# GpSimd in VectorE's place: the low part of the split weights, from the input projection to the output projection

## What is computed

```python
def first_block(x, ...):
    n = _rms(h, norm_mix_w[l])
    z = n @ w_in[l]                                  # (528, 1024) @ (1024, 7168)
    q, k, v, glu, g_att, g_conv = jnp.split(z, splits, axis=-1)
    ...
    o = _diff_attention(q, k, v, lam, cid)           # 8 heads, two softmaxes each
    y_att = (_rms(o, subln_w[l]) * (1.0 - lambda_init)).reshape(b, lp, ATT_V)
    u = glu[..., :CONV_CH] * jax.nn.sigmoid(glu[..., CONV_CH:])
    u = _causal_dwconv(u, conv_dw_w[l], conv_dw_b[l])   # 31 taps over 1024 channels
    u = jax.nn.silu(_layernorm(u, conv_ln_w[l], conv_ln_b[l]))
    y_conv = u @ w_conv_out[l]
    m = jax.nn.sigmoid(g_att) * y_att + jax.nn.sigmoid(g_conv) * y_conv
    h = h + m @ w_out[l]
    ...
    # then a gated feed-forward with 3-tap convolutions, a norm,
    # and two layers of short convolution and retention (second_block)
```

## Time and profile before

| | us |
|---|---|
| median of 3 runs | 1806.2 |
| lowest and highest of them | 1805.16, 1809.17 |
| the profiled execution, its own time | 1807.76 |
| its span, first to last instruction | 1806.0 |
| TensorE busy | 1787.0 (99%) |
| VectorE busy | 1403.3 (78%) |
| ScalarE busy | 967.9 (54%) |
| GpSimd busy | 164.6 (9%) |
| mean granted TensorE clock | 0.998 of full speed |

### The profile page before, as it was taken

How to read it: one execution, slowest core, us unless ns; L and a number is a source line. 1 busy time by engine, 2 the same in 40 slices (tenths; PEclk the granted TensorE clock), 3 DMA queues, 4 the chain that set the end, 5 groups by cost and what they waited for, 6 DMA issues and landing times.

```text
span 1806.0 us, 31948 instructions
## 1 busy us (share of the span) xinstructions
PE 1787.0 (99%) x13222; PEld 1687.2 (93%) x13222; DVE 1403.3 (78%) x2464; ACT 967.9 (54%) x1894; POOL 164.6 (9%) x138
## 2 busy tenths in 40 slices
PE   9999999999999999999999999999999999999998
PEld 8999999978899989999889999999898999999987
DVE  5888898578756789969878996899357898689844
ACT  6223332568734446547556665667346566566632
POOL 0000000000000012011001211120000122122000
PEclk9999999999999999999999999999999999999999
DMA  5222222200132257566346876785332677577531
GB/s 193 96 75 93 94 86 80 94 24 25 64 107 73 80 136 165 133 160 144 108 117 146 173 159 139 157 170 127 117 94 71 127 167 161 139 156 168 124 117 70
DMA packets 247679, 213.42 MB, mean 118 GB/s; under 512 B 6646, under 2 KB 239919, under 8 KB 247534
## 3 DMA queue, kind: packets, MB, share of 16 engines
q1 hardware_dynamic: 180990, 178.34, 32.2%
q0 software_dynamic: 66528, 33.04, 14.9%
q10 hardware_dynamic: 16, 0.00, 0.0%
HBM read 209.26 MB, written 2.10 MB: 117 GB/s over the span
## 4 chain that ended last, share of the span: by engine, by line
PE 88%; DVE 6%; ACT 4%; DMA 1%; issue 1%; SPq 0%; DVEq 0%; ACTq 0%
PE ps L664 41%; PE ps L705 29%; PE ps L1313 6%; PE ps L1362 5%; DVE wlo L2350 2%; PE ps L893 1%; PE ps L1151 1%; PE ps L1126 1%; ACT p L1624 1%; ACT whi L1396 1%; DMA raw<-in_w_up_dram 1%; PE ps L1142 1%; PE ps L1154 1%; PE ps L918 1%; DVE y L2846 0%
## 5 line engine op out<-in xcount | busy, mean ns | idle before, releaser
L2350 DVE TENSOR_TENSOR wlo<-raw,whi 128x1024 fp32r<-128x1024 f32 (+1 forms) x363 | 438.7, 1214 | 203.9 <-ACT whi L1396 203.0
L1396 ACT ACTIVATE whi<-raw 128x1024 fp32r<-128x1024 f32 (+1 forms) x363 | 380.8, 1052 | 253.3 <-PE ps L664 107.1
L664 PE MATMUL ps<-nhi,whi 128*128 128x256 f32 (+3 forms) x1392 | 315.9, 290 | 1.5 <-DVE clo L2618 0.8
L664 PE MATMUL ps<-nhi,wlo 128*128 128x256 f32 (+3 forms) x1392 | 311.8, 288 | 0.0
L664 PE MATMUL ps<-nlo,whi 128*128 128x256 f32 (+2 forms) x1264 | 275.0, 287 | 0.0
L664 PEld LDWEIGHTS ps<-nhi,whi 128*128 128x128 f32 x1392 | 226.8, 189 | 5.2 <-DVE clo L2618 1.0
L664 PEld LDWEIGHTS ps<-nhi,wlo 128*128 128x128 f32 x1392 | 225.8, 189 | 2.1
L705 PE MATMUL ps<-thi,whi 128*128 128x256 f32 x784 | 225.2, 287 | 2.1 <-DVE wlo L2350 0.7
L705 PE MATMUL ps<-thi,wlo 128*128 128x256 f32 x784 | 221.6, 283 | 0.0
L705 PE MATMUL ps<-tlo,whi 128*128 128x256 f32 x784 | 221.4, 282 | 0.0
L705 PE MATMUL ps<-nhi,whi 128*128 128x256 f32 (+1 forms) x756 | 215.8, 285 | 0.0
(11 more groups left out here) (473 smaller groups left out, 3604.1 us busy)
## 6 DMA issues: line engine op xcount, KB each, us to landing
raw<-in_w_in_dram SPq DMA_DIRECT2D x90, 1024.0 KB, 5.9
raw<-in_w_up_dram SPq DMA_DIRECT2D x22, 1024.0 KB, 5.1
raw<-in_w_out_dram SPq DMA_DIRECT2D x20, 1024.0 KB, 5.1
s1t<-in_w_in_dram SPq DMA_DIRECT2D x49, 256.0 KB, 3.5
s1t<-in_w_in_dram POOLq DMA_DIRECT2D x49, 256.0 KB, 7.1
raw<-in_w_in_dram POOLq DMA_DIRECT2D x49, 256.0 KB, 4.7
raw<-in_w_down_dram SPq DMA_DIRECT2D x16, 512.0 KB, 3.4
raw<-in_w_conv_out_dram SPq DMA_DIRECT2D x4, 1024.0 KB, 5.2
```

Source lines behind the costliest of these rows:

```text
L664: mm = eng.matmul(o, w, m[:, k, a:b], start=begins, stop=final and n == len(ks) - 1 and i == 2)
L1396: eng.activation(hi, raw, ACT.Copy).then_inc(*A.up("hi", s))
L2350: eng.tensor_tensor(lo, raw, hi.bitcast(F), ALU.subtract).then_inc(*V.up("lo", s))
```

## The change

A set of slots, `BY_GPSIMD`, is defined: from 4 up to the first slot of the feed-forward, 72 (68 slots). For these VectorE's `low(s)` returns at once, and GpSimd makes the same subtraction of the same operands, `G("lo", s)`, after `A("hi", s)`. The two waits on the low part, TensorE's in `products` and SyncE's before a load, ask the function `low_in` which engine made it. GpSimd's zeroing of `v` and of the two small tiles keeps its waits and now stands between the subtractions of slots 25 and 26, and of 57 and 58.

```diff
+        BY_GPSIMD = range(4, next(r for r, (u, _, _) in enumerate(slots) if u == first_ffn))
...
+        def low_in(s):
+            return G("lo", s) if s in BY_GPSIMD else V("lo", s)
+
         def tensor_program(eng):
...
                                 if n == c == i == j == 0:
-                                    on.wait_ge(V("lo", s))
+                                    on.wait_ge(low_in(s))
...
             def low(s):
+                if s in BY_GPSIMD:
+                    return
                 u, n, _ = box_of(s)
                 hi, lo, raw = split_views(s)
                 on.wait_ge(A("hi", s))
...
-            on.wait_ge(T("keys"), A("square_x", 0))
-            eng.memset(V_[:, 0, :], 0.0).then_inc(*G.up("meta"))
-            for i in range(2):
-                on.wait_ge(T("gate", 15))
-                eng.memset(AT[i][:, 4, :], 0.0).then_inc(*G.up("at_rows", i))
+
+            for s in BY_GPSIMD:
+                u = slots[s][0]
+                if s == slots.index((12, BY_COL[0], False)) + 2:
+                    on.wait_ge(T("keys"), A("square_x", 0))
+                    eng.memset(V_[:, 0, :], 0.0).then_inc(*G.up("meta"))
+                elif s == slots.index((28, BY_COL[0], False)) + 2:
+                    for i in range(2):
+                        on.wait_ge(T("gate", 15))
+                        eng.memset(AT[i][:, 4, :], 0.0).then_inc(*G.up("at_rows", i))
+                hi, lo, raw = split_views(s)
+                on.wait_ge(A("hi", s))
+                eng.tensor_tensor(lo, raw, hi.bitcast(F), ALU.subtract).then_inc(*G.up("lo", s))
...
                     if n > 1:
                         on.wait_ge(V("second_sum", sevens[n - 2]), V("lo", slot_of[sevens[n - 2], 1]))
-                    on.wait_ge(V("lo", raw2_read))
+                    on.wait_ge(low_in(raw2_read))
...
                 if final and v:
-                    on.wait_ge(V("lo", s))
+                    on.wait_ge(low_in(s))
```

## The result

| | before | after |
|---|---|---|
| median of the runs shown now, us | 1807.41 | 1823.26 |
| lowest of them, us | 1805.16 | 1821.48 |
| the profiled execution, its own time, us | 1807.76 | 1822.59 |
| its span, us | 1806.0 | 1820.8 |

The ratio is 1.0085, with a 95% interval of 1.0065 to 1.0105: the change costs some 0.85%. Forecast were 1828 (21.9 us more) and slower. One of the four runs of after, 1851.82, was disturbed and is left out of the ratio; the median of the other three is 1822.59, 15.2 us above before.

What follows compares the result with a forecast made beforehand. TensorE, busy 99% of the span, was taken to bound the kernel. Mean 14.1, clock 1.5 and attention 6.3 sum to 21.9 us, which on the 1806.2 median makes 1828; range 1804 to 1845.

Steps and rivals of the forecast that it cites:

- the term that decided: Convolution and attention: GpSimd's and VectorE's two-input SBUF instructions exclude each other, 2.3 us held per subtraction; chance 0.62.
- the memset: Six taps beside a GpSimd memset kept 4.07 us, so its writes do not slow VectorE; its reads stayed untested.
- no harm: Rival: engines share SBUF freely or VectorE loses under 2 us per subtraction; 1805 to 1808, chance 0.25.
- faster: Rival: attention's 4.4 us of TensorE idle all come from VectorE and vanish; 1801.8, chance 0.08.
- VectorE never lets go: Rival: GpSimd's subtractions wait behind 60 taps in one piece, three pieces costing 30 us each; 1890, chance 0.05.
- GpSimd's subtraction, 2.25 us: Estimated length of one 1024-column GpSimd subtraction, priced from its memset and one-input instruction; bounds 1.23 and 2.9 us.
- Held per subtraction, 2.3 us: VectorE blocked 2.25 us plus 0.05 for the change of hands; TensorE then waits 14.1 us at the mean.
- The prediction's own formula: VectorE's work up to the mean, 128.5 + 33 g + (61.94 - 13.8 + 12 g - 72), against 194 us; g is time held.
- the threshold of 2.0: Time held per subtraction, in us, from which VectorE's lateness costs TensorE anything at the mean.
- The clock, 1.5 us: Behind the stall at the mean the granted clock may fall once, 3 us at 1.2 GHz, losing 1.5 us.
- Attention, 0.9 us a head: GpSimd's reading delays `p`, VectorE's chain has 1.9 more and 1.15 less; 6.3 us over seven heads.
- What cost nothing: Costed at nothing: GpSimd's lateness to TensorE, SyncE's loads 1.1 us later, and VectorE's lighter list before the mean.

Runs made afterwards that it cites:

- nobody: Changed kernel with the low parts of slots 4 to 71 made by no engine: 1805.98 us against 1806.72, ratio 0.9995.
- quarters: Changed kernel with each GpSimd subtraction split into four instructions of 256 elements a row: 1809.74 us against 1805.16, ratio 1.0025.
- Twice as many: Changed kernel with each GpSimd subtraction in slots 4 to 57 made two times, one after the other: 1929.89 us against 1805.16, ratio 1.0692.
- Paced: Changed kernel, but VectorE still waits for each high part where its own subtraction used to stand: 1827.28 us against 1807.48, ratio 1.0117.
- input only: Changed kernel with only the slots before 58 (input projection and gates) on GpSimd: 1811.97 us against 1806.72, ratio 1.0026.
- Attention only: Changed kernel with only the slots from 58 on (attention and output projection) on GpSimd: 1818.77 us against 1806.72, ratio 1.0064.
- attention late: Kernel with only slots from 58 on GpSimd; the heads' subtractions wait for VectorE's largest score: 1815.28 us against 1807.48, ratio 1.0047.
- the copy: Changed kernel with GpSimd copying the raw weights (one input) in place of subtracting: 1870.25 us against 1805.16, ratio 1.0359.
- every other: Changed kernel with alternate pairs of slots 4 to 57 on GpSimd, the rest back on VectorE: 1807.32 us against 1805.16, ratio 1.0012.

## Why the prediction was right where it was, and where not

**Direction and mechanism: right.** TensorE's full list left nothing to gain (*nobody*: 0.9995), and GpSimd's subtraction and VectorE's two-input instructions exclude each other, which was the term that decided. That for instructions with two inputs it is reading that excludes, as argued from the memset, is shown by the kernel that only writes. Of the rivals *no harm* and *faster* are out. *VectorE never lets go* is not what set the time of this kernel, but it is real: one subtraction in the changed kernel shows it.

```profile
245.40 10.72 DVE L2527 SCALAR_TENSOR_TENSOR c<-u,cv,c 128x514 f32<-128x514 f32 x16
...
256.42 2.15 DVE L2563 TENSOR_TENSOR lam<-lam 128x64 f32<-128x64 f32 x1
...
248.15 12.69 POOL L3518 TENSOR_TENSOR wlo<-raw,whi 128x1024 fp32r<-128x1024 f32 x2 [3.42 <-ACT whi L1401]
```

The first of the two took 10.33 us: VectorE ran some 12 of these 16 taps past it, at 0.67 us each, and came to two pairs of small instructions (two inputs, then a reduction of one). At the first pair GpSimd still waited, at the second it had its turn and held `lam` for 1.9 us. The subtraction queued behind it ran mostly while VectorE waited for ScalarE, and held it for 0.4. That the delay cost TensorE 0.5 us and not 30 was luck of the place.

**GpSimd's subtraction, 2.25 us (estimate): 2.39 alone.** A miss of 0.14, and an avoidable one: the prediction's own terms, 2.2 ns for each of 1024 columns and 85 ns fixed, make 2.34; it left the 85 ns out and then took 2.25 without a reason. The price of the second input, taken from the first one's, was good.

**Held per subtraction, 2.3 us: 2.06. The mis-sized term at the mean.** VectorE is busy 195.2 us between 114 and 311 us (taps, sums and held time); less the 127.2 of its own work in *nobody* that is 68.0 us, over 33 subtractions 2.06. A held tap stands for 2.14 us, less than the 2.39 of the subtraction, since a part of GpSimd's duration does not hold VectorE; and the one behind the subtraction that was passed over held next to nothing. The prediction's own formula with 2.06 instead of 2.3 gives 45 x 2.06 - 89.4 = 3.3 us at the mean, against 14.1 forecast and 3.4 measured. That agreement is a weak test, since the 2.06 is read from the very time that VectorE was busy. The quarters test the threshold of 2.0 better: their 1.95 is read from the taps alone, and the mean did not wait. Twice as many gave 101.4 for 96, in part by other waits. The prediction named the threshold and a range from 2.05 to 2.7 for the time held, and 2.06 lies at its very edge: a term that moves 45 us for each microsecond of its one estimated input was almost nothing.

**The clock, 1.5 us: 3.0** (6.4 less 3.4; the expectations say 2.6, from a matmul that was not yet through). Towards the end of the stall, from 310.2 on, the granted clock fell, as it had after the thin stretch near the start:

```profile
307.00:312.00 5.00, 2.14 (x12) 1.75 (x12) 3.83 (x3) 0.00 (x0) 3.32 (x1) 0.82 0.20 69
312.00:317.00 5.00, 5.00 (x23) 4.81 (x22) 1.29 (x2) 0.00 (x0) 0.00 (x0) 0.50 0.02 3
```

In before these stretches are at 1.00. At 0.50, that is 1.2 GHz, 5 us pass with 23 matmuls, where before had 44. The stall of 3 us brought 6.8 us at half clock and not the 3 us that the prediction took from the start, so the term was too small, and it did not need a stall of 14 us. *Paced* (6.8 us) and *input only* (3.4 us) show a drop at the same place, and of the kernels in which the mean did not wait none does. What sets its length is open: *input only* has the longer stall and the shorter drop.

**Attention, 0.9 us a head, 6.3 in all: 1.5 a head, 11.8 in all.** The second mis-sized term, in the other direction. Timelines of after in the head before that of the earlier trace rows (the five full heads are alike, 16.16 us each):

```profile
430.01 2.36 POOL L3518 TENSOR_TENSOR wlo<-raw,whi 128x1024 fp32r<-128x1024 f32 x1 [13.79 <-ACT whi L1401]
...
430.13 2.26 DVE L2651 SCALAR_TENSOR_TENSOR ast<-ast,neglam 128x1 f32<-128x1 f32 x1
...
434.06 0.68 DVE L2675 TENSOR_TENSOR m<-m,ga 128x514 f32<-128x514 f32 x1
435.26 0.17 DVE L2647 RECIPROCAL ast<-ast 128x2 f32<-128x2 f32 x1 [0.52 <-ACT p L1629]
```

The instruction ahead of `p`, 0.22 us before, takes 2.26: held for 2.04, close to the 1.9 forecast. TensorE loses 1.0 us at the turn of this `p`, as the prediction's 0.9 had it; the other 0.5 us are lost later in the head, at the next turn (0.2) and at the scores that wait for ScalarE (0.3), and for these the prediction has no term. It counted VectorE's chain as 1.9 more and 1.15 less, for the subtraction that left it. Here `m` with `ga` ends at 434.74 and VectorE stands idle for 0.52 us until ScalarE's exponentials are there: the subtraction had stood in time in which the chain would wait for ScalarE anyway. From one reciprocal to the next it is 5.31 us, before 3.81 (433.72 to 437.53): 2.04 more, 1.15 less, and 0.6 of the 1.15 lost again as that wait (0.52) and around it. The same prediction had said, a few steps earlier, that taking the subtraction off the chain gives TensorE 0.05 to 0.2 us a head (*nobody*: 0.19), and then credited 1.15. Besides, the five full heads make 7.6 us of the 11.8; 2.9 us come between the end of the drop and the first of them, and 1.3 behind the last, where other instructions with two inputs are held as well (the chain has one `ast` of 1.69 us at 381.00 and an `rcol` of 2.27 at 494.87, against 0.2 each). *Attention only* against *attention late* shows the mechanism in a head; how the 2.9 us come together was not tested.

**What cost nothing: right.** GpSimd's lateness reached TensorE for 0.5 us, SyncE's loads for nothing that shows, leaving VectorE paid nothing before the mean.

**The sum.** 14.1 + 1.5 + 6.3 = 21.9 forecast; 3.4 + 3.0 + 11.8 = 18.2 measured at the end of attention, 14.8 in the span for the reason given above. The total is nearer than its terms, since two errors have opposite signs: that part of the agreement is luck. In the section on what would show each step, two signs held in kind (taps of up to 3 us, a wait at the mean), one in size was off by a factor of four (14 us at the mean), and heads of 15.5 us are 16.15.

## What to carry to other kernels

Work moved from VectorE to GpSimd isn't parallel if VectorE's instructions read two tensors of SBUF and GpSimd's reads SBUF too, be it one tensor: count what a GpSimd instruction holds (here 2.06 us, for 1.15 us saved) against VectorE's room up to the next point that TensorE waits for, and where that sum has a threshold near the estimate, take the forecast from the estimate's range and not from its middle. An instruction that stands beside another engine's wait is worth less when it leaves a chain than it costs when it enters it elsewhere. And look at what the move takes from VectorE's list besides the work: with its waits gone, VectorE runs in long rows, and a GpSimd instruction can be passed over until the row ends, which one wait per tile prevented.

## What the runs showed of the hardware that I had not expected

**GpSimd can be passed over for as long as VectorE has instructions that exclude it.** 10.3 us in the changed kernel, 35.4, 35.1 and 16.7 us with the copy and 5.3 to 6.7 us four times more, 35.8 and 7.8 us with twice as many subtractions, 9.0 to 10.5 us five times in *every other*. The copy showed it in seven of 68, the subtraction in one of 68 here, the quarters not once (none of the 272 is over 1.30 us). I looked at where within a tap GpSimd arrived: in the changed kernel it was passed over at 0.10 us and not at 0.08, 0.09 or 0.12, and the copies that were passed over arrived between 0.10 and 0.47 us, so the place within a tap does not decide it. What decides whether it gets in at the next change of instructions or never is open.

**A VectorE instruction with a single tensor input is held too, if it is a multiplication by scalars.** The first taps, 0.54 us before and in most cases after:

```profile
L2524 DVE TENSOR_SCALAR c<-u,cv x8: 537/544/2627, 43.4 to 244.9; 128x514 f32<-128x514 f32 x8
L2554 DVE TENSOR_TENSOR u<-ps,sg x8: 690/694/708, 41.6 to 113.4; 128x528 f32<-128x528 f32 x8
```

One of the eight, at 242.39, took 2.63 us. GpSimd's writes hold such an instruction as well (above). The product `ps * sg`, which has one of its two inputs in PSUM, never was held, though five of the eight ran beside a subtraction, and neither were the reciprocals, of which 13 in six kernels began inside one and took 0.17 us at most. An instruction on 128 x 1 elements is held as long as one on 128 x 514 (2.26 us against 0.22).

**The hold does not scale away.** 1.04 us alone and 0.87 held for the copy, 2.39 and 2.14 for the subtraction, 0.74 and 0.49 for a quarter of it: in all three VectorE is held for 0.17 to 0.25 us less than the instruction lasts alone. So four quarters hold 1.95 us although they last 2.96 alone.
